# The sums over the weights woven into the raw chunks' products, and mean and variance at other places of TensorE's order

## The chip, the cores and the metric

The kernel runs on one core of one Trainium2 chip. A core has a matrix engine (TensorE, called PE in the profile; its loads of weights are called PEld), a vector engine (VectorE, DVE), an engine for functions (ScalarE, ACT), a general one (GpSimd, POOL) and one that issues the transfers (SyncE, SP). The metric is the time of one execution on the device in microseconds. Three runs of the kernel before gave 3748.06, 3753.95 and 3755.0 us, so the median is 3753.95 us.

## The reference

Two models of two layers each run one after the other on a sequence of 512 tokens of width 1024. In the first, each layer has a gated feed-forward block, a token mixer and a second feed-forward block; behind each stands a layer norm, whose result is scaled and shifted by a modulation for the next block:

```
y = _swiglu(_modulate(x, sh1, sc1), ffn1_w_gate[l], ffn1_w_up[l], ffn1_w_down[l])
x = _post_norm(x, y, g1, FFN_RES, ln_gain[l, 0], ln_bias[l, 0])      # layer norm of ALPHA*x + res_w*(1+gate)*y
y = _token_mixer(_modulate(x, sh2, sc2), w_in[l], w_out[l])
...
mu = jnp.mean(xf, -1, keepdims=True)
var = jnp.mean(jnp.square(xf - mu), -1, keepdims=True)
y = (xf - mu) * lax.rsqrt(var + LN_EPS)
```

The first model has six such norms. The change touches five: all but the last, which is followed by the second model and goes another way. What follows each of the five is a product of the modulated norm with a weight matrix, and this is what the kernel starts early: with A the product of gain and scale, and B that of bias, scale and shift, the product of h = A (x - mu) r + B with W is r (W'(A x) - mu W'A) + W'B. W'(A x) needs neither mean nor variance, and W'A and W'B are two sums over the weights per output column.

## The kernel before, in words

All activations lie transposed in the core's memory: 8 row tiles of 128 features by 512 tokens. Weights come in chunks of 8 x 128 rows by 256 columns (1 MB) into a ring of three staging tiles (`s_stage`). ScalarE rounds a chunk to its high part (`s_wh`, L1714), VectorE subtracts this from the chunk and so makes the low part (`s_wl`, L2039); activations are split the same way (`s_hh`, `s_hl`, and `s_ah`, `s_al`). A product is three products of parts, each of 512 columns (L1361, for all of TensorE's products go through one helper). The step `mm2` takes a chunk's two output tiles together: for each row tile k it issues 2 x 3 products into two banks.

A planner (class `Plan`) writes a list of steps. Each engine walks through that one list and issues its own part of each step, so the order in the list is the order on every engine. `tick()` lets background work (attention, tables) put in steps of its own. `late` (L339) is the planner's part for one of the five norms. It takes two weight chunks, `one` and `two` (gate and up of the feed-forward block, or two chunks of `w_in`), whose products are made of the raw A x (tiles `s_ah`, `s_al`), while mean and variance are still on their way. In TensorE's order there stand:

- four row tiles of `one` (24 products), `ln_mean` (one fp32 product of the running sum with a constant, 2 passes of 512 columns), the other four row tiles;
- `sums` (the step `uv`, L1487) for the first output tile of `one`: for each k an fp32 product of the raw chunk in the staging tile with two columns, A and B (2 passes each, 128x2); then `ln_var` (16 passes with one column); then `sums` for the second output tile;
- two row tiles of `two`, `ln_spread` (the reciprocal root over all 128 rows, 8 passes), the other six row tiles, and `sums` for both output tiles of `two`.

VectorE subtracts the mean from the eight tiles (`ln_sub`, L2123), ScalarE squares them, POOL and VectorE add the squares up (L2118), VectorE splits the next chunk (L2039), takes the root (`ln_root`, from L2014), splits another chunk, multiplies by the root and makes the first four tiles of h (`ln_h`, L2153, L2159, L2032), reads the sums (`uv_out`, L2134 and L2136), corrects the two raw tiles of `one` (`late`, L2143 and L2146), makes the other four tiles of h and corrects those of `two`. ScalarE copies the raw tiles out of the banks (`late_copy`, L1714 with `s_tmp<-ps`), then rounds a chunk. The running sum that the mean needs is kept by POOL (L2580). A staging tile is free for its next transfer once the low part is made and, for the two raw chunks, once the sums are read.

Here is the code that the change touches.

## Time and profile before

| | us |
|---|---|
| median of the three runs | 3753.95 |
| the profiled execution's own time | 3751.07 |
| its span (first to last instruction) | 3749.8 |
| TensorE products busy | 3607.5 (96%), 16972 |
| TensorE weight loads busy | 2925.8 (78%) |
| VectorE busy | 1844.1 (49%) |
| ScalarE busy | 1267.9 (34%) |
| POOL busy | 517.8 (14%) |
| small products of the raw chunks with the coefficients (`ps<-s_sm,s_stage`) | 43.1, 320 passes, 267 ns mean |
| ScalarE's rounding of a chunk (`s_wh`, L1714), mean of one | 1.876 |
| VectorE's split of a chunk (`s_wl`, L2039), mean of one | 2.190 |
| granted TensorE clock, mean of the span | 0.965 |

Busy times are sums over an engine's instructions and overlap between engines. Products are pipelined: one of 512 columns shows 0.39 us, but the next starts 0.23 us after it, so the distance from start to start is what a product costs. The granted clock is a share of full speed: 1.00 is 2.4 GHz, 0.50 is 1.2 GHz. "Idle before" names what ended an engine's wait.

### The profile page before, as it was taken

The numbers are of one execution on the slowest core, as the hardware profiler recorded it, in microseconds if no ns is written. First come the engines' busy times: TensorE is split into PE (matmuls) and PEld (weight loads), VectorE is DVE, ScalarE is ACT, GpSimd is POOL, SyncE is SP. The second block draws the span as 40 slices with busy tenths as digits, with TensorE's granted clock in tenths as the row PEclk, the third lists the DMA queues.
The fourth block names the chain that finished last, engine by engine and source line by source line (L and its number), as shares of the span: only waits on it lengthen the run. The fifth ranks groups of instructions, "written<-read, shape, count | busy, mean of one in ns | idle before, by whom it ended". The sixth has DMA issues, their size and how long they took to land. (4 is left out here: it accounts for less than half of the span.)

```text
span 3749.8 us, 41532 instructions
## 1 busy us (share of the span) xinstructions
PE 3607.5 (96%) x16972; PEld 2925.8 (78%) x16972; DVE 1844.1 (49%) x3196; ACT 1267.9 (34%) x1722; POOL 517.8 (14%) x448
## 2 busy tenths in 40 slices
PE   8999989999999999999999989988999999999999
PEld 7888867688888888867788877646878887787887
DVE  4545653665546544644643244775543334564332
ACT  2222461342224222552342233334442223343222
POOL 1010220110012000211210011111121111202111
PEclk9999999999999999999999989969999999999999
DMA  6444222134443443210132221101212222222222
GB/s 247 164 150 154 105 83 86 46 110 171 147 146 109 170 148 134 80 57 34 55 112 91 97 76 67 58 1 35 90 68 94 97 101 82 90 79 79 101 95 74
DMA packets 52609, 373.45 MB, mean 100 GB/s; under 512 B 5826, under 2 KB 5954, under 8 KB 9539
## 3 DMA queue, kind: packets, MB, share of 16 engines
q1 hardware_dynamic: 52418, 370.79, 27.6%
q8 instruction: 134, 2.20, 0.2%
q14 instruction: 57, 0.46, 0.0%
HBM read 368.67 MB, written 2.10 MB: 99 GB/s over the span
## 5 line engine op out<-in xcount | busy, mean ns | idle before, releaser
L1361 PE MATMUL ps<-s_hh,s_wh 128*128 128x512 f32 x2680 | 1069.5, 399 | 43.6 <-DVE s_wl L2039 16.4
L1361 PE MATMUL ps<-s_hl,s_wh 128*128 128x512 f32 x2680 | 1052.5, 393 | 0.0
L1361 PE MATMUL ps<-s_hh,s_wl 128*128 128x512 f32 x2680 | 1051.5, 392 | 0.0
L2039 DVE TENSOR_TENSOR s_wl<-s_stage,s_wh 128x2048 fp32r<-128x2048 f32 (+2 forms) x288 | 630.4, 2190 | 635.5 <-ACT s_wh L1714 635.3
L1714 ACT ACTIVATE s_wh<-s_stage 128x2048 fp32r<-128x2048 f32 (+1 forms) x277 | 519.7, 1876 | 629.2 <-PE ps L1361 500.9
L1361 PEld LDWEIGHTS ps<-s_hh,s_wh 128*128 128x128 f32 x2680 | 507.6, 189 | 180.5 <-issue 48.2
L1361 PEld LDWEIGHTS ps<-s_hh,s_wl 128*128 128x128 f32 x2680 | 507.5, 189 | 109.8
L1361 PEld LDWEIGHTS ps<-s_hl,s_wh 128*128 128x128 f32 x2680 | 508.2, 190 | 105.1 <-issue 2.1
L1361 PE MATMUL ps<-s_ah,s_wh 128*128 128x512 f32 x1376 | 544.8, 396 | 0.0
L1361 PE MATMUL ps<-s_al,s_wh 128*128 128x512 f32 x1376 | 539.9, 392 | 0.0
L1361 PE MATMUL ps<-s_ah,s_wl 128*128 128x512 f32 x1376 | 539.7, 392 | 0.0
L2615 POOL TENSOR_TENSOR s_al<-s_tmp,s_ah 128x512 fp32r<-128x512 f32 x152 | 196.7, 1295 | 1684.2 <-ACT s_ah L1714 1684.2
L1361 PEld LDWEIGHTS ps<-s_ah,s_wl 128*128 128x128 f32 x1376 | 261.0, 190 | 55.6
L1361 PEld LDWEIGHTS ps<-s_al,s_wh 128*128 128x128 f32 x1376 | 261.2, 190 | 54.9 <-issue 1.2
L1361 PEld LDWEIGHTS ps<-s_ah,s_wh 128*128 128x128 f32 x1376 | 261.2, 190 | 54.7 <-issue 1.2
L1738 ACT ACTIVATE s_tmp<-ps 128x512 f32<-128x512 f32 x146 | 87.1, 596 | 438.6 <-PE ps L1361 438.5
L1714 ACT ACTIVATE s_ah<-s_tmp 128x512 fp32r<-128x512 f32 x152 | 96.1, 632 | 407.9 <-DVE s_tmp L2234 342.8
L2092 DVE TENSOR_TENSOR s_xr<-ps,s_xr 128x512 f32<-128x512 f32 x96 | 66.2, 690 | 231.0 <-PE ps L1361 231.0
L2090 DVE SCALAR_TENSOR_TENSOR s_xr<-ps,s_sm,s_xr 128x512 f32<-128x512 f32 x112 | 83.9, 749 | 169.0 <-PE ps L1361 168.7
L2055 DVE SCALAR_TENSOR_TENSOR s_tmp<-s_stage,s_cond,s_tmp 128x256 f32<-128x256 f32 x378 | 155.3, 478 | 0.0
L2234 DVE TENSOR_TENSOR s_tmp<-s_tmp,ps 128x512 f32<-128x512 f32 x82 | 56.1, 685 | 147.9 <-PE ps L1361 147.8
L2220 DVE TENSOR_TENSOR s_tmp<-s_tmp 128x512 f32<-128x512 f32 x64 | 47.1, 736 | 165.5 <-ACT s_tmp L1738 165.4
(428 smaller groups left out, 3649.8 us busy)
## 6 DMA issues: line engine op xcount, KB each, us to landing
s_stage<-in_w_ada SPq DMA_DIRECT2D x64, 1024.0 KB, 4.8
s_stage<-in_ffn_w_gate SPq DMA_DIRECT2D x44, 1024.0 KB, 4.8
s_stage<-in_ffn_w_up SPq DMA_DIRECT2D x44, 1024.0 KB, 4.8
s_stage<-in_ffn_down SPq DMA_DIRECT2D x32, 1024.0 KB, 4.8
s_stage<-in_w_up SPq DMA_DIRECT2D x32, 1024.0 KB, 4.8
s_stage<-in_down_m SPq DMA_DIRECT2D x32, 1024.0 KB, 4.8
s_stage<-in_w_in SPq DMA_DIRECT2D x24, 1024.0 KB, 4.8
s_stage<-in_ffn_down SPq DMA_DIRECT2D x16, 768.0 KB, 4.2
```

The costliest lines, as they stand in the source:

```text
L1361: return pe.matmul(out, lhs, rhs, start=start, stop=stop, skip_group_check=True)
L1714: return act.activation(out, src, ACT.Copy)
L1738: act.activation(m.tmp(q), m.bank(b), ACT.Silu if kind == "swiglu" else ACT.Relu).then_inc(*e.up("act_ffn", "act", pid))
L2039: ins = dve.tensor_tensor(m.WL[:, ws, a:z], m.STAGE[:, j % NS, a:z], m.WH[:, ws, a:z].bitcast(F32), ALU.subtract)
L2055: ins = dve.scalar_tensor_tensor(dst, w[:, k, :], cond, dst, ALU.mult, ALU.add)
L2090: ins = dve.scalar_tensor_tensor(x, m.bank(b), m.small(gate[0])[:, n:n + 1], x, ALU.mult, ALU.add)
L2092: ins = dve.tensor_tensor(x, m.bank(b), x, ALU.add)
L2220: dve.tensor_tensor(m.tmp(q), m.tmp(q), m.tmp(q), ALU.mult).then_inc(*e.up("dve_ffn", "act.sq", pid))
L2234: dve.tensor_tensor(m.tmp(q), m.tmp(q), m.bank(b), ALU.mult).then_inc(*e.up("dve_ffn", "glu", pid))
L2615: pool.tensor_tensor(m.AL[a][:, k, :], m.tmp(q), m.AH[a][:, k, :].bitcast(F32), ALU.subtract).then_inc(*e.up("pool_a", "a.lo", av, k))
```

## The change

The sums over the weights are no longer steps of their own. `mm2` gets a further argument, and behind the six products of a row tile k it issues that row tile's share of both sums (`weight_sums`): four passes of two columns, whose weights are the raw chunk. So the 32 passes of a chunk come in eight groups of four. `ln_mean` moves from behind row tile 3 of `one` to behind row tile 1, and `ln_var` now follows the last row tile of `one` with no sums around it. `uv_out` of `one` is read ahead of `ln_root` and no longer behind the first half of `ln_h`. As the part of `one` is now handed out in three pieces and not in two, `tick()` is called once more in each of the five norms.

```diff
-        def part(ch, pid, kt, n, bs, x, ver, ks, i0, i1):
-            self.add("mm2", pid, ch, kt, n, bs, x, ver, ks, i0, i1)
+        def part(which, ch, pid, kt, n, bs, x, ver, ks, i0, i1):
+            self.add("mm2", pid, ch, kt, n, bs, x, ver, ks, i0, i1, 0, (sid, s, uv, which))
             self.tick()
-
-        def sums(ch, i, t):
-            self.add("uv", sid, ch, s, uv, i, t)
...
-        def finish(ch, i, mean, rs):
-            self.add("uv_out", sid, ch, i, uv, su)
+        def finish(i, mean, rs):
...
-        part(*one, 0, 4)
+        part(0, *one, 0, 2)
         mean = self.banks.take()
         self.add("ln_mean", sid, norm.acc, mean)
         self.tmp.free(norm.acc, ("ln.mean", sid))
-        part(*one, 4, 8)
+        part(0, *one, 2, 4)
+        part(0, *one, 4, 8)
...
         if low:
             self.add("low", *low)
-        sums(one[0], 0, 0)
         self.add("ln_var", sid, sq, var)
         for n in (3, 7):
             self.tmp.free(sq[n], ("ln.var", sid))
-        sums(one[0], 0, 1)
         self.release(one[0], ("proj", one[1] + 1))
         copies(one, 0)
+        self.add("uv_out", sid, one[0], 0, uv, su)
...
-        finish(one[0], 0, mean, rs)
-        part(*two, 4, 8)
+        finish(0, mean, rs)
+        part(1, *two, 4, 8)
         self.add("ln_h", sid, rs, s, self.hfree, self.hv, qs, 4, NT)
-        for t in range(2):
-            sums(two[0], 1, t)
         self.release(two[0], ("proj", two[1] + 1))
         copies(two, 1)
-        finish(two[0], 1, mean, rs)
+        self.add("uv_out", sid, two[0], 1, uv, su)
+        finish(1, mean, rs)
...
+            if uv:
+                weight_sums(ch, k, i == 0, i == kt - 1, *uv)
+
+    def weight_sums(ch, k, start, stop, sid, s, b, which):
+
+        w = m.STAGE[:, ch.j % NS, :].rearrange("p (k n) -> p k n", k=NT)
+        if start:
+            e.wait_ge(("ln.c", sid, 3), ("uv.out", sid, 0) if which else b.after)
+        for t in range(2):
+            at = 4 * which + 2 * t
+            ins = mul(m.bank(b)[:, at:at + 2], w[:, k, t * P:(t + 1) * P], m.small(s)[:, k:k + 9:8], start and t == 0, stop)
+        if stop:
+            ins.then_inc(*e.up("pe_uv", "uv", ch.j))
```

On TensorE, at the end of chunk `one` in the first of the five norms, there stand before (`s_sm,s_stage` are the sums, `s_cc,s_tmp 128x1` the variance, `s_ah`/`s_al` with `s_wh`/`s_wl` the raw products; here each product of fp32 counts once, in the trace it is two passes):

```order
L1361 MATMUL ps<-s_ah_70,s_wl 128x512
L1361 MATMUL ps<-s_sm,s_stage 128x2 [waits q_dve_mod]
L1361 MATMUL ps<-s_sm,s_stage 128x2 x7
L1361 MATMUL ps<-s_cc,s_tmp 128x1 [waits q_pool_sum]
L1361 MATMUL ps<-s_cc,s_tmp 128x1 x3
L1361 MATMUL ps<-s_cc,s_tmp 128x1 [waits q_dve_fold]
L1361 MATMUL ps<-s_cc,s_tmp 128x1 x3
L1361 MATMUL ps<-s_sm,s_stage 128x2 x8
L1361 MATMUL ps<-s_ah_70,s_wh 128x512 [waits q_dve_x6,q_dve_x5,q_dve_w]
```

At the same place, on TensorE, there stand now:

```order
L1356 MATMUL ps<-s_ah_70,s_wl 128x512
L1356 MATMUL ps<-s_sm,s_stage 128x2 x2
L1356 MATMUL ps<-s_cc,s_tmp 128x1 [waits q_pool_sum]
L1356 MATMUL ps<-s_cc,s_tmp 128x1 x3
L1356 MATMUL ps<-s_cc,s_tmp 128x1 [waits q_dve_fold]
L1356 MATMUL ps<-s_cc,s_tmp 128x1 x3
L1356 MATMUL ps<-s_ah_70,s_wh 128x512 [waits q_dve_x6,q_dve_x5,q_dve_w]
```

Of the 16 products for the sums two are left at this place; the others stand behind the earlier row tiles, and the ones for `two` likewise.

On TensorE, around the mean of the same norm (`s_tmp,s_cc 128x512`), there stand now two row tiles of `one` ahead of it, each with its two products for the sums; before, it stood behind four row tiles and with no sums between:

```order
L1356 MATMUL ps<-s_sm,s_stage 128x2 [waits q_dve_mod]
L1356 MATMUL ps<-s_sm,s_stage 128x2
L1356 MATMUL ps<-s_ah_70,s_wh 128x512 [waits q_dve_h]
L1356 MATMUL ps<-s_al_71,s_wh 128x512
L1356 MATMUL ps<-s_ah_70,s_wl 128x512
L1356 MATMUL ps<-s_ah_70,s_wh 128x512
L1356 MATMUL ps<-s_al_71,s_wh 128x512
L1356 MATMUL ps<-s_ah_70,s_wl 128x512
L1356 MATMUL ps<-s_sm,s_stage 128x2 x2
L1356 MATMUL ps<-s_tmp,s_cc 128x512 [waits q_dve_x4,q_pool_sum]
```

The mean thus moved ahead of two row tiles (12 products), and its own waits stay the same.

On VectorE, from the last fold of the squares to the root of the same norm, the two copies of the sums move in (a piece of the difference):

```order
 L2039 TENSOR_TENSOR s_wl<-s_stage,s_wh 128x2048
+L2134 TENSOR_SCALAR s_sm<-ps 128x2
+L2136 COPY s_sm<-ps 128x2
 L2014 TENSOR_SCALAR s_nv<-ps 128x4
 L2016 TENSOR_SCALAR s_nu<-s_nv 128x4
```

They stood between the first half of `ln_h` and the corrections of `one`. The orders of ScalarE, POOL and SyncE are the same as before.

## Rows read from the trace of the kernel before

**Rows 1.** Timeline of TensorE, norm one: start us, us, what, [idle before].

```profile
417.56 1.02 PE L1361 MATMUL ps<-s_tmp,s_cc 128*128 128x512 f32 x2
...
418.65 0.39 PE L1361 MATMUL ps<-s_al,s_wh 128*128 128x512 f32 x1
...
423.90 1.84 PE L1361 MATMUL ps<-s_sm,s_stage 128*128 128x2 f32 x16
...
427.35 1.05 PE L1361 MATMUL ps<-s_cc,s_tmp 128*128 128x1 f32 x8 [0.71 <-DVE s_tmp L2118]
...
430.89 0.77 PE L1361 MATMUL ps<-s_ah,s_wh 128*128 128x512 f32 x1
...
436.07 1.05 PE L1361 MATMUL ps<-s_cc,s_ny 128*128 128x128 f32 x8
...
445.17 3.63 PE L1361 MATMUL ps<-s_sm,s_stage 128*128 128x2 f32 x32
448.66 0.37 PE L1361 MATMUL ps<-s_wh,s_hh 128*128 128x256 f32 x1
```

**Rows 2.** TensorE in windows: stretch us, busy (count), granted clock, DMA share, GB/s.

```profile
429.00:436.00 7.00, 7.00 (x23) 0.51 0.42 150
449.00:453.00 4.00, 3.96 (x22) 0.58 0.75 291
...
545.00:549.00 4.00, 4.00 (x11) 0.57 0.02 6
2692.00:2697.00 5.00, 5.00 (x31) 1.00 0.63 211
```

**Rows 3.** Windows of 35 us, all engines, norms three and four.

```profile
1143.00:1178.00 35.00, 35.00 (x178) 30.27 (x177) 29.82 (x53) 18.40 (x26) 8.99 (x7) 0.85 0.20 74
1529.00:1564.00 35.00, 35.00 (x183) 30.92 (x182) 27.80 (x49) 17.29 (x25) 8.05 (x7) 0.83 0.15 46
```

**Rows 4.** Timeline of VectorE: first subtraction and first multiply of the norms.

```profile
418.62 0.69 DVE L2123 TENSOR_TENSOR s_xr<-s_xr,ps 128x512 f32<-128x512 f32 x1 [3.62 <-PE ps L1361]
437.16 0.69 DVE L2153 TENSOR_TENSOR s_xr<-s_xr,ps 128x512 f32<-128x512 f32 x1 [3.21 <-PE ps L1361]
775.07 0.69 DVE L2153 TENSOR_TENSOR s_xr<-s_xr,ps 128x512 f32<-128x512 f32 x1 [4.82 <-PE ps L1361]
1143.36 1.28 DVE L2123 TENSOR_TENSOR s_xr<-s_xr,ps 128x512 f32<-128x512 f32 x2 [3.62 <-PE ps L1361]
1161.07 0.69 DVE L2153 TENSOR_TENSOR s_xr<-s_xr,ps 128x512 f32<-128x512 f32 x1 [3.23 <-PE ps L1361]
1549.39 0.69 DVE L2153 TENSOR_TENSOR s_xr<-s_xr,ps 128x512 f32<-128x512 f32 x1 [4.71 <-PE ps L1361]
```

**Rows 5.** Timelines of POOL and TensorE behind the raw chunks, norms one and three.

```profile
451.44 1.28 POOL L2566 TENSOR_TENSOR s_hl<-s_tmp,s_hh 128x512 fp32r<-128x512 f32 x1 [1.08 <-ACT s_hh L1777]
...
1186.76 0.50 PE L1361 MATMUL ps<-s_hh,s_wh 128*128 128x512 f32 x1 [1.43 <-DVE s_wl L2039]
```

**Rows 6.** Timeline of TensorE: four small passes between products, and sixteen.

```profile
2610.76 0.50 PE L1361 MATMUL ps<-s_cc,s_tmp 128*128 128x1 f32 x4
...
2611.45 0.40 PE L1361 MATMUL ps<-s_hl,s_wh 128*128 128x512 f32 x1
...
2692.27 1.95 PE L1361 MATMUL ps<-s_cc,s_ny 128*128 128x128 f32 x16
```

**Rows 7.** Timelines of POOL and VectorE, norm one.

```profile
413.15 1.29 POOL L2580 TENSOR_TENSOR s_tmp<-s_tmp,s_xr 128x512 f32<-128x512 f32 x1 [1.32 <-DVE s_xr L2090]
...
442.49 0.15 DVE L2134 TENSOR_SCALAR s_sm<-ps 128x2 f32<-128x2 f32 x1
```

**Rows 8.** Timeline of ScalarE: copies of the raw tiles, norms one and three.

```profile
427.39 1.09 ACT L1714 ACTIVATE s_tmp<-ps 128x512 f32<-128x512 f32 x2 [1.54 <-DVE s_tmp L2118]
...
1152.39 1.09 ACT L1714 ACTIVATE s_tmp<-ps 128x512 f32<-128x512 f32 x2 [3.49 <-PE ps L1361]
```

**Rows 9.** Timeline of TensorE: a long stall in the attention of layer one.

```profile
544.75 1.68 PE L1361 MATMUL ps<-s_nk,s_cc 128*128 128x384 f32 x3 [2.95 <-POOL s_nk L2627]
```

More of the change, by code:

```diff
@@ L386, in late @@
             self.tmp.free(sq[n], ("ln.var", sid))
-        sums(one[0], 0, 1)
         self.release(one[0], ("proj", one[1] + 1))
         copies(one, 0)
+        self.add("uv_out", sid, one[0], 0, uv, su)
         low = self.ahead()
         two = self.begin(self.take(*names[1], ada=False, late=True), 8, S, "g", sid)
-        part(*two, 0, 2)
+        part(1, *two, 0, 2)
         y, rs = self.yr.take(), self.banks.take()
@@ L399, in late @@
         self.yr.free(y, ("ln.rs", sid))
-        part(*two, 2, 4)
+        part(1, *two, 2, 4)
         self.hv += 1
@@ L1407, in mm, with mm2 @@
             ins.then_inc(*e.up("pe_proj", "proj", pid))
-    def mm2(pid, ch, kt, N, bs, x, ver, ks, i0, i1, wait=0):
+    def mm2(pid, ch, kt, N, bs, x, ver, ks, i0, i1, wait=0, uv=None):
         wh, wl = weights(ch, kt, 256)
@@ L1485, in ln_var @@
         ins.then_inc(*e.up("pe_norm", "ln.var", sid))
-    def uv(sid, ch, s, b, i, t):
-        w, at = m.STAGE[:, ch.j % NS, :].rearrange("p (k n) -> p k n", k=NT), 4 * i + 2 * t
-        e.wait_ge(("ln.c", sid, 3), ("uv.out", sid, 0) if i else b.after)
-        for k in range(NT):
-            ins = mul(m.bank(b)[:, at:at + 2], w[:, k, t * P:(t + 1) * P], m.small(s)[:, k:k + 9:8], k == 0, k == NT - 1)
-        if t == 1:
-            ins.then_inc(*e.up("pe_uv", "uv", ch.j))
     def ln_spread(sid, y, rs):
@@ L1692, in tensor @@
     run(plan, dict(
-        mm=mm, mm2=mm2, mmt=mmt, ada_pe=ada_pe, ada_sum=ada_sum, ln_mean=ln_mean, ln_var=ln_var, uv=uv,
+        mm=mm, mm2=mm2, mmt=mmt, ada_pe=ada_pe, ada_sum=ada_sum, ln_mean=ln_mean, ln_var=ln_var,
         ln_spread=ln_spread, ln_a=ln_a, ln_last=ln_last, rms_a=rms_a, rms_b=rms_b, m_rope=m_rope, sb_z=sb_z, sb_sum=sb_sum,
```

## The prediction

> **What bounds the kernel now.** I read the page first, then TensorE's own timeline at the five layer norms that the change touches (they begin near 418, 754, 1143, 1530 and 1846 us; I call them norms one to five), then the granted clock of those stretches, then VectorE and ScalarE beside them. The page says that TensorE is busy for 96% of the span, so a change pays if it takes work off TensorE, makes that work run faster, or closes a stall. In norm one [rows 1] the reader is to see five things in order: the mean (two passes, 417.56), then 24 products of 512 columns, then a heap of small passes from 423.90 to 430.89 (16 for the sums over the weights, 16 for the variance with a wait of 0.71 us in them, 16 more for the sums), then twelve products that take 436.07 - 430.89 = 5.2 us where 24 of them took 423.90 - 418.65 + 0.23 = 5.5 us ahead of the heap (0.2275 each), then the spread of the reciprocal root at 436.07. After 36 more products a second heap of 32 passes takes 448.66 - 445.17 = 3.49 us.
>
> The windows [rows 2] say why: behind the first heap the granted clock is 0.51 for 7 us, which is the lower of the two levels (1.2 and not 2.4 GHz), and behind the second heap 0.58 over 4 us. TensorE was not idle ahead of either fall but for the 0.71 us; it ran small passes. All five norms have it: over 35 us each the mean clock is 0.85 in norm three and 0.83 in norm four [rows 3] (one and five are like three, two like four), which is (1 - 0.85) x 35 = 5.2 and 6 us of full clock lost.
>
> That is not yet what can be won, since VectorE's chain (subtract the mean, squares, variance, root, normalise, write h) hangs on TensorE at two places, mean and spread: it waits 3.62 us for the mean and 3.2 to 4.8 us for the spread in each norm [rows 4]. And what TensorE does after the two raw chunks needs that chain: in norm one the next product waits for the last h tile (POOL until 452.72), in norm three it waits 1.43 us at 1186.76 for weights that VectorE split late [rows 5]. So I count how much earlier VectorE gets its mean and its spread.
>
> **Removed, added, moved.** The number of passes is the same: 320 small ones of two columns (43.1 us busy in the table), 32 to a chunk, ten chunks. They now come in 16 groups of four per norm in place of heaps of 16, 16 and 32. Price of a group of four [rows 6]: without it the two products behind it would start 0.23 us apart, with it 2611.45 - 2610.76 = 0.69, so 0.46 us, or 0.116 a pass. The heap of 32 costs 3.49 [rows 1], or 0.109 a pass. So a group costs some 0.02 us beyond its passes, and there are 13 more groups in a norm than heaps: 65 x 0.02 = 1.3 us, all inside the sums below. These rows have other operands (a constant and a statistics tile); no row shows fp32 weights from the staging tile in fours. Bounds: from below, the first load hidden behind the product before, 0.1 us less a group (80 x 0.1 = 8 us less work); from above, twice the row, 0.9. I take the row, as the passes of both kinds show the same length in a heap of 16 (1.84 for the sums, 1.95 for a spread) [rows 1, 6].
>
> The Trainium skill (TensorE: Matmul & The Clock Gate, What happens when you issue a matmul) says that the weights of the next tile load while the running matmul streams. By that a group standing behind a long product would hide its first load, which a heap hides once for 16; the page alone would put the groups at the lower bound just named. The rows show no such discount (0.116 a pass in fours, 0.109 in thirty-two), so I don't take it.
>
> The mean moves from behind 24 products to behind 12 products and two groups: 12 x 0.2275 - 2 x 0.46 = 1.8 us earlier. It can: it needs the last running sum, which POOL finishes at 414.44 in norm one, and the mean would be at 417.56 - 1.8 = 415.8 [rows 7]. No queue of SP, ACT or POOL changes its order; on VectorE only the two small copies of the sums move ahead of the root, where VectorE has just finished a split of weights and waits for the variance; at 0.15 us each, overlapping a little, they free 0.25 us later in the chain [rows 7].
>
> From the new mean, with the clock full: mean 418.65 - 417.56 - 0.23 = 0.86; 36 products 8.19; six groups 2.78; variance 16 passes 1.75, without the 0.71 us wait, as the folds now end 1.8 us earlier and TensorE comes later: 13.6 us to the end of the variance (in norm one its second half began 427.35 - 417.56 = 9.8 after the mean and took 0.9, so 10.7, so the root starts later relative to the mean, which is the price of putting sums ahead of it). Then 12 products and two groups, 3.66: the spread starts 17.3 us after the mean, against 436.07 - 417.56 = 18.5. VectorE's first multiply follows the spread by 437.16 - 436.07 = 1.09, so it lies 17.3 us behind VectorE's first subtraction (itself 1.06 behind the mean). Before, that distance was 437.16 - 418.62 = 18.54 in norm one and 17.71 in norm three (and five, which is like it); norm two waits 4.82 for the spread and not 3.21 as norm one, so 20.15, and norm four 4.71 and not 3.23 as norm three, so 19.2 [rows 4].
>
> What is late next: in norms three to five the copies of the raw products on ScalarE wait for the variance, and not in norms one and two (1152.39 "PE", 427.39 "DVE") [rows 8]. Behind the variance stand there some 0.2 us until the copies start, 1.09 for them, 1.9 for ScalarE's rounding of a chunk and 2.2 for VectorE's split of it (both by their means in the table), 5.4 in all against the 4.75 of the spread: the distance is 17.95 in these three.
>
> Gain per norm, at VectorE's first multiply: 1.8 + 18.54 - 17.3 = 3.0; 1.8 + 20.15 - 17.3 = 4.65; 1.8 + 17.71 - 17.95 = 1.55; 1.8 + 19.2 - 17.95 = 3.05; 1.55. Sum 13.8, and with 0.25 each 15.1 us. TensorE itself would be 3.7 us and more ahead (the heap of 3.49 us becomes six groups, 2.78, and 3.4 us at half clock behind it go), but it meets the h tiles and the late weights, so the smaller number counts and the rest turns into stalls.
>
> Two terms go the other way. First, the last group and the variance still stand together: 20 small passes, 2.2 us. Sixteen together left the clock at 1.00 (2692.27, window from 2692) [rows 2, 6]; thirty-two brought it down (window from 449: (1 - 0.58) x 4 = 1.7 us of full clock lost, 3.4 us at the lower level) [rows 2]; twenty are not shown. Such a half stretch costs 1.7 us, of which norms three to five hide 0.65: 6.6 us if it comes everywhere, 0 if nowhere; I take half, 3.3. Second, the new stalls: in norms two, three and five the wait for weights grows from 1.4 to some 4 us, in one and four some 2 us of waits for h tiles arise. A stall of 2.95 us was followed by a clock of 0.57 over 4 us, again 1.7 us lost [rows 2, 9]. Up to 1.7 us each in four norms (norm three has another such wait 12 us later that hides it): 0 to 6.8, I take 2.5. In all 15.1 - 3.3 - 2.5 = 9.3 us.
>
> One small thing more: each norm now hands the background work one turn more, which moves a few small instructions of the fifth by twelve products; between -0.5 and +0.5 us, taken as 0.
>
> The profiled execution took 3751.07 us, 2.9 under the median of the three runs and 1.2 under their mean (3752.3). I set the gain against that mean: 3743.
>
> **The rivals.**
> (B) The half clock stays in another place: it comes behind all five bursts of twenty and all four new stalls. For it: heaps of 32 did it in all five norms, and so did the stall of 2.95 us [rows 9]. Against it: sixteen passes did not. 15.1 - 6.6 - 6.8 = 1.7 us gained: 3750.6, no change that can be told (about 0.2%, 7.5 us, is what a measurement of this kernel can tell).
> (C) The clock holds everywhere, 15.1 us gained: 3737. For it: between two groups stand six full products. Against it: the burst of twenty.
> (D) Slower: a group in fours costs far more than the row, since fp32 passes from the staging tile stand between fp32r products and each change of kind costs a drained array. For it: no row has these operands in fours. Against it: other small passes cost 0.46 in fours, the way back to products included [rows 6]. Ten groups stand between the first raw product and the spread on the chain, fifty in all; 15.1 us are gone when a group costs 0.30 us more than the row, and at 0.9 us (the upper bound) 50 x 0.44 = 22 us are lost against 15.1 gained: 3759.
> That the change does not do what it says (the sums would wait for a coefficient or a bank at the new place) I exclude: the coefficients are needed by the raw products anyway.
>
> (E) The clock falls between mean and spread exactly as it does now, because what brings it down is not the heaping of small passes but something that the change leaves in place. For it: nothing in one trace tells the two apart. Against it: each of the ten heaps has its own fall behind it (two in norm one) [rows 2]. Then 3.4 us are lost in norms one, three and five and 5.1 in two and four, as now, and the distances are 17.3 + 3.4 = 20.7 and 17.3 + 5.1 = 22.4: the sum of 1.8 + (distance before) - (distance after) is -4.8, with the 1.25 of the moved copies -3.5, so 3755.8.
>
> The Trainium skill (TensorE: Matmul & The Clock Gate, Why this matters for your kernels) puts a clock that drops in mid-kernel down to idle gaps between matmul bursts; by that rule the busy heaps would not be the cause and (E) would be the case. The clock falls behind the second heap too, ahead of which TensorE was busy without a wait [rows 1, 2], so the trace disagrees.
>
> **How the numbers follow.** Main case 0.47, 3743, its own range 3738 to 3748; (B) 0.20; (C) 0.18; (D) 0.10; (E) 0.05. Faster by over 0.2%, that is below 3745: all of C and two thirds of the main case, 0.50. Slower: D, 0.10. The rest, 0.40, within 0.2%. Range 3734 to 3756: it takes in C, the main case, B, E and the near side of D.
>
> **What would show each step.** Small passes in fours that lengthen the distance of two products to 0.69 us; the first subtraction 1.8 us nearer to the raw products; a clock of 1.00 between mean and spread or one half stretch of 3.4 us, and none where the heap of 32 stood; VectorE's distance of 17.3 us in norms one and two and 18 in three to five; a wait of some 4 us for weights in norms two, three and five. I am wrong if the distance stays at 18 to 20, if a group costs over 0.6 us, or if the time won at the norms comes back as waits further on.

## The result, and the profile after

The changed kernel took 3743.94 us (median of 13 runs, 3740.87 to 3751.33) where the kernel before took 3753.19 beside it: ratio 0.9979, 95% interval [0.9970, 0.9987]. Timed again later it was 0.9974 [0.9963, 0.9984] (3744.04 us, 7 runs). So it is faster by 0.2 to 0.3%. The forecast was 3743. All ratios here compare fast runs alone, so they differ a little from the quotient of two medians (0.9975 here), and one run of the kernel before that took 8327 us is in none of them.

Norm one on TensorE in the changed kernel, its small passes, with the products around the first group of four (columns as in [rows 1]):

```profile
413.54 0.39 PE L1356 MATMUL ps<-s_ah,s_wl 128*128 128x512 f32 x1
413.77 0.50 PE L1356 MATMUL ps<-s_sm,s_stage 128*128 128x2 f32 x4
...
414.45 0.40 PE L1356 MATMUL ps<-s_al,s_wh 128*128 128x512 f32 x1
...
415.97 1.10 PE L1356 MATMUL ps<-s_tmp,s_cc 128*128 128x512 f32 x2
...
427.43 0.50 PE L1356 MATMUL ps<-s_sm,s_stage 128*128 128x2 f32 x4
427.79 1.93 PE L1356 MATMUL ps<-s_cc,s_tmp 128*128 128x1 f32 x16
431.83 0.84 PE L1356 MATMUL ps<-s_sm,s_stage 128*128 128x2 f32 x4
...
434.84 1.14 PE L1356 MATMUL ps<-s_cc,s_ny 128*128 128x128 f32 x8
```

From the start of a group of four to the start of the second product behind it there are 414.45 - 413.77 = 0.68 us, as [rows 6] had it (0.69). The burst of twenty is there at 427.43. Behind it one group takes 0.84 in place of 0.50: the clock is down. The windows of TensorE in the same kernel (stretch, busy and count, granted clock, DMA share, GB/s; the answer to [rows 2, 3]) show where it falls now:

```profile
430.00:434.00 4.00, 4.00 (x14) 0.57 0.54 227
449.00:453.00 4.00, 2.80 (x19) 1.00 1.00 424
...
792.00:795.50 3.50, 3.50 (x10) 0.52 0.76 250
...
1178.00:1184.00 6.00, 5.58 (x13) 0.50 0.73 247
1514.00:1549.00 35.00, 35.00 (x198) 1.00 0.09 32
...
1878.00:1884.00 6.00, 5.53 (x13) 0.50 0.57 186
```

One half stretch of 3.4 us behind the burst of twenty in norm one (two and three have it too), none in norms four and five, none where the heap of 32 stood. In norm four the clock is 1.00 over 35 us where it was 0.83. But at 792, 1178 and 1878 us it is at the lower level. The kernel before has full clock behind the same products (norms two, three and five):

```profile
801.00:805.00 4.00, 4.00 (x18) 1.00 0.76 264
1187.00:1191.00 4.00, 4.00 (x19) 1.00 0.87 274
1890.00:1894.00 4.00, 4.00 (x19) 1.00 0.73 262
```

What stands there is the wait for late weights, grown from 1.43 us [rows 5], in TensorE's timeline of the changed kernel:

```profile
791.71 0.61 PE L1356 MATMUL ps<-s_hh,s_wh 128*128 128x512 f32 x1 [3.55 <-DVE s_wl L2039]
...
1178.42 0.80 PE L1356 MATMUL ps<-s_hh,s_wh 128*128 128x512 f32 x1 [3.53 <-DVE s_wl L2039]
...
1878.47 0.79 PE L1356 MATMUL ps<-s_hh,s_wh 128*128 128x512 f32 x1 [3.64 <-DVE s_wl L2039]
```

VectorE, the answer to [rows 4]: first subtraction and first multiply of norm one, then those of norm four, whose multiply shows no wait for TensorE:

```profile
417.12 1.28 DVE L2123 TENSOR_TENSOR s_xr<-s_xr,ps 128x512 f32<-128x512 f32 x2 [1.85 <-PE ps L1356]
436.02 0.69 DVE L2153 TENSOR_TENSOR s_xr<-s_xr,ps 128x512 f32<-128x512 f32 x1 [1.65 <-PE ps L1356]
...
1521.05 1.28 DVE L2123 TENSOR_TENSOR s_xr<-s_xr,ps 128x512 f32<-128x512 f32 x2 [1.85 <-PE ps L1356]
1538.88 0.68 DVE L2153 TENSOR_TENSOR s_xr<-s_xr,ps 128x512 f32<-128x512 f32 x1
```

Why the weights are late shows in norm two (VectorE, then ScalarE, same kernel): VectorE's split waits 2.50 us for ScalarE's rounding of the same weights, and ScalarE starts that at 787.44, behind its last tile of the raw products' silu.

```profile
789.37 2.29 DVE L2039 TENSOR_TENSOR s_wl<-s_stage,s_wh 128x2048 fp32r<-128x2048 f32 x1 [2.50 <-ACT s_wh L1714]
```

```profile
786.90 0.63 ACT L1714 ACTIVATE s_ah<-s_tmp 128x512 fp32r<-128x512 f32 x1 [1.33 <-DVE s_tmp L2224]
787.44 1.89 ACT L1714 ACTIVATE s_wh<-s_stage 128x2048 fp32r<-128x2048 f32 x1
```

Behind norm four, in the attention of layer two, one more half stretch stands that the kernel before has not: TensorE waits 1.79 us for a tile of POOL (1589.97), and then the clock is at the lower level, in the second timed execution too (1596.80:1600.00, 0.50). The kernel before waits there as long (1601.09, 1.72 us) and stays at full clock (1601.00:1605.00, 1.00). Changed kernel:

```profile
1590.80:1594.00 3.20, 3.20 (x9) 0.50 0.02 5
```

Last, the span cut at the first product of each norm's raw chunk, TensorE's windows. Kernel before:

```profile
412.12:748.43 336.31, 312.39 (x1588) 0.93 0.21 76
748.43:1136.86 388.43, 386.33 (x1755) 0.98 0.39 141
1136.86:1523.58 386.72, 383.87 (x1747) 0.99 0.39 139
1523.58:1839.88 316.30, 302.99 (x1555) 0.95 0.15 54
```

The changed kernel:

```profile
412.40:742.69 330.29, 305.40 (x1587) 0.96 0.21 77
742.69:1129.40 386.71, 383.16 (x1756) 0.99 0.39 142
1129.40:1516.34 386.94, 383.41 (x1748) 0.99 0.38 139
1516.34:1830.52 314.18, 299.30 (x1555) 0.96 0.15 54
```

The changed kernel in the second timing, another execution of the same program:

```profile
412.00:748.58 336.58, 312.12 (x1588) 0.94 0.21 76
748.58:1135.27 386.69, 383.13 (x1755) 0.99 0.39 142
1135.27:1522.30 387.03, 383.50 (x1747) 0.99 0.38 139
1522.30:1836.51 314.21, 299.35 (x1556) 0.96 0.15 54
```

The reader is to see two things. Stretches two to four repeat to 0.1 us between the two executions of the changed kernel, and there it gains 1.7, -0.2 or -0.3, and 2.1 us. The first stretch does not repeat: 330.29 and 336.58. It holds norm one and the attention of layer one, with its many short waits. By the starts of the same product, before less changed, norm one ends (477 us) 1.5 and 1.7 us ahead in the two executions, and at 559 us, in the attention, they are 3.2 ahead and 0.2 behind. What is apart there is the granted clock (0.96 and 0.94), and no instruction of the change stands there. So some 4 of the 9.2 us between the first two traces are no effect that can be put down to a place. The whole span of the second execution is 3746.5 us, only 3.3 under the kernel before. Other stretches can scatter too: in two executions of the kernel with only the mean moved (below) the stretch of norm four, with the attention of layer two, took 317.0 and 313.2 us.

### The profile page after: what moved, and what is told of

The parts are those of the page before. It is cut to its first block, busy times and chain, and to the rows that moved or that the text cites. A ratio compares the mean times of both kernels' runs of the same rounds, so it can differ in the third digit from the quotient of the medians.

```text
span 3740.6 us, 41529 instructions
## 1 busy us (share of the span) xinstructions
PE 3592.7 (96%) x16972; PEld 2912.7 (78%) x16972; DVE 1843.8 (49%) x3196; ACT 1268.0 (34%) x1722; POOL 517.8 (14%) x448
## 4 chain that ended last, share of the span: by engine, by line
PE 43%; DVE 5%; ACT 2%; issue 1%; POOL 0%; DVEq 0%; ACTq 0%; POOLq 0%
PE ps L1356 42%; DVE s_wl L2039 1%; ACT s_wh L1714 0%; ACT s_tmp L1867 0%; DVE s_tmp L2313 0%; PE ps L1381 0%; DVE s_hl L2032 0%; DVE s_tmp L2303 0%; DVE s_tmp L2209 0%; DVE s_sm L2311 0%; ACT s_hh L1714 0%; DVE s_gc L2489 0%; DVE s_tmp L2436 0%; DVE s_sm L2416 0%; DVE s_bm L2418 0%
```

## The experiments

Each is timed against the kernel before on the same chip. The experiments ran on three chips, so kernels of different experiments are best compared by their ratios. All results at a glance:

| kernel | median us (runs) | ratio, 95% interval |
|---|---|---|
| changed, again | 3744.04 (7) | 0.9974 [0.9963, 0.9984] |
| only the mean moved | 3747.24 (11) | 0.9981 [0.9972, 0.9990] |
| the same, again | 3748.09 (11) | 0.9984 [0.9975, 0.9993] |
| only the sums woven | 3754.33 (12) | 1.0005 [0.9997, 1.0014] |
| changed, a quarter of the sums' passes | 3737.31 (5) | 0.9954 [0.9942, 0.9966] |
| changed, weights split early | 3736.65 (6) | 0.9947 [0.9933, 0.9961] |
| mean moved in norms one, two only | 3750.14 (12) | 0.9999 [0.9987, 1.0011] |
| before, chunk in three parts | 3751.57 (12) | 0.9996 [0.9986, 1.0006] |
| mean moved, weights split early | 3745.10 (12) | 0.9986 [0.9976, 0.9996] |
| changed, variance in halves | 3740.44 (5) | 0.9958 [0.9945, 0.9972] |
| changed, variance in halves and weights split early | 3725.36 (6) | 0.9932 [0.9918, 0.9947] |

**The change taken apart.** My theory was that weaving brings most of the gain, by keeping the clock up, and the mean's move little.

Only the mean moved:

```diff
-        part(*one, 0, 4)
+        part(*one, 0, 2)
...
         self.add("ln_mean", sid, norm.acc, mean)
...
+        part(*one, 2, 4)
         part(*one, 4, 8)
```

> The kernel before with one edit: the mean stands behind two row tiles of the first raw chunk and no longer behind four; the sums stay in their heaps of 16, 16 and 32 passes. Theory (the gain of the change comes from the earlier mean and the full clock together, and neither alone carries it): VectorE's first subtraction comes 12 x 0.2275 = 2.7 us earlier against the raw chunk, but the 12 products now stand behind the mean, so the variance and the spread stay where they were on TensorE; only the wait of 0.71 us inside the heap goes in norms one and two, and the half clock behind both heaps stays. Gain 1.4 us in all, ratio to before 0.9996, no difference that can be told; distance from first subtraction to first multiply 20.5 us in norm one where it was 18.5. Rival (the earlier mean is what wins the time, the weaving is idle): five times 1.8 to 2.7 us, 9 to 13 us, ratio 0.997.

Measured 0.9981: the theory's number is missed, the rival's is met. The mean comes 5.44 - 2.72 = 2.7 us earlier, the folds come in time, and the variance no longer waits in the heap. Below are TensorE's heaps of norm two in this kernel, and the clock behind them:

```profile
756.62 1.84 PE L1362 MATMUL ps<-s_sm,s_stage 128*128 128x2 f32 x16
758.32 2.12 PE L1362 MATMUL ps<-s_cc,s_tmp 128*128 128x1 f32 x16
760.30 3.55 PE L1362 MATMUL ps<-s_sm,s_stage 128*128 128x2 f32 x16
```

```profile
759.00:767.00 8.00, 8.00 (x36) 0.57 0.25 80
```

Half stretches stay behind both heaps. What the trace shows as gained is the wait of 0.71 us in the heaps of norms one [rows 1] and two, and one half stretch fewer between mean and spread in norms one, two and four (one more in norm three). In a second execution of this kernel norm one has as much of it as before; two, three and four are as here.

Only the sums woven, the mean in its old place:

```diff
         part(0, *one, 0, 2)
+        part(0, *one, 2, 4)
...
         self.add("ln_mean", sid, norm.acc, mean)
...
-        part(0, *one, 2, 4)
         part(0, *one, 4, 8)
```

> The changed kernel with one edit: the mean goes back behind four row tiles of the first raw chunk; the sums stay woven in groups of four. Theory: the mean comes 7.3 us after the start of the raw chunk where the changed kernel has 3.6, the squares are summed 9.7 us after it, TensorE gets to the variance after 8.2 and waits 1.5 us, with half of the variance done in the wait; the multiply comes 22.8 us after the start of the raw chunk at full clock and 24.5 with one half stretch behind the variance, where it was 25.1 in norm one, 26.7 in two, 24.2 in three and five and 25.7 in four before, and is 22.0 to 23.6 in the changed kernel. Gain 3 to 7 us against before, ratio 0.9985, that is about half of the change. Rival (the weaving alone does it, the place of the mean is idle): the ratio of the changed kernel, 0.9979. Rival (the earlier mean does it): 1.000.

Measured 1.0005: missed as well. In norm one of this kernel four groups stand ahead of the mean, which comes 7.23 us behind the raw chunk's start and not 5.44, and the folds, later by as much, are waited for:

```profile
419.69 1.11 PE L1356 MATMUL ps<-s_tmp,s_cc 128*128 128x512 f32 x2
...
429.56 1.67 PE L1356 MATMUL ps<-s_cc,s_tmp 128*128 128x1 f32 x8 [0.67 <-DVE s_tmp L2118]
```

The clock does not hold either: between mean and spread it is at the lower level for 6.8 us in norms one to three and 3.4 in four and five, and behind the variance TensorE waits 0.5 to 1.15 us in each norm for weights that VectorE, now later, splits later. Sum by places: VectorE's first multiply is 26.4 us behind the raw chunk's start against 25.0 before in norm one, and 24.7 against 25.8 in norm four; the stalls for the weights are 3.5 us all the same, with half clock behind them. So the mean alone gives some 6 us, the weaving alone none, both together 8 to 10. The reading that fits the traces is that the earlier mean pays for the groups ahead of it, and the weaving needs the earlier mean. But the intervals of the mean alone and of both overlap, so what weaving adds in this setting is not shown.

**What limits the change.** Two candidates: the price of the groups, and the stall behind the norms.

The sums at row tiles 0 and 7 only (240 of the 320 passes are left out, so the sums are incomplete):

```diff
-            if uv:
+            if uv and i in (0, kt - 1):
                 weight_sums(ch, k, i == 0, i == kt - 1, *uv)
```

> The changed kernel, and of the eight groups of four small passes of each raw chunk only the first and the last are issued: six of eight row tiles are left out of the two sums over the weights, so 240 of 320 passes go. It measures what a group costs on the chain. Theory (a group costs 0.46 us on TensorE, and TensorE sets the mean and the spread): of the ten groups ahead of the spread seven go (row tile 0 and 7 of the first chunk and row tile 0 of the second stay), 3.2 us; the multiply comes up to 3.2 us earlier in each norm, less where ScalarE's copies and rounding set it; the 20 passes around the variance stay and with them the chance of a half stretch. 8 to 16 us faster than the changed kernel, ratio to before 0.994 to 0.996. Rival (a group in fours with fp32 weights from the staging tile costs 0.9 us): 25 to 30 us faster, 0.990. Rival (groups are hidden, the chain sits elsewhere): within 2 us of the changed kernel, 0.998.

Measured 0.9954 [0.9942, 0.9966], in the range of the ratio that the theory gave; the gain over the changed kernel is 6.6 us by the medians and 9 by the ratios, at the lower end of the 8 to 16 expected. The 240 passes are 60 groups, so 60 x 0.46 = 28 us of TensorE's time went, and only a quarter to a third of it came out as time. VectorE's multiply comes 13.0 us earlier over the five norms, but TensorE then waits behind the variance (0.67 us in norms one and two) and at the h tiles (1.74 and 1.21 us in norm one), and the stall for weights stays (3.64 us in norm two). So the groups do cost something, and most of what they cost is hidden.

The weights behind the norms split early. This adds one item to the order, so that ScalarE's rounding and VectorE's split of the next chunk stand ahead of the raw products' silu:

```diff
                     one, two, afree[1] = self.late(norm, ((names["gate"], idx), (names["up"], idx)))
+                    low = self.ahead()
+                    if low:
+                        self.add("low", *low)
```

> The changed kernel with one edit: in the three norms in front of a feed-forward block, the chunk that TensorE waits for after the third (3.5 us in norms two, three and five) is rounded and split right behind the raw chunks, ahead of the activation and the parts of the first output tiles, and not behind them. Theory (what the change won at the norms is partly given back by this wait and by the half clock behind it): ScalarE's rounding comes some 7 us earlier, the wait of 3.5 us goes in norms two and five, in norm three at least in part (its next chunk is behind a transfer), and so does the half stretch that follows it (lost clock 1.7, 3.4 and 3.4 us there). Gain over the changed kernel 3 x 3.5 + 3 to 5 = 8 to 15 us, ratio to before 0.994 to 0.996. Rival (the wait is only moved: the activation and its parts come later and TensorE waits for them or for the transfer): ratio 0.998 as the changed kernel.

Measured 0.9947 [0.9933, 0.9961], in the expected range: 7 us under the changed kernel by the medians (just short of the 8 expected) and 12 by the ratios, for an edit without any work less. Its six runs lie from 3725.9 to 3741.6 us, and the profiled one is the fastest, so the trace as a whole flatters it; single stretches tell more. The stretch of norm two has no stall and only the half stretch behind the burst of twenty (first row); in norm three, where the chunk behind the next is one of modulation weights, which is not split this way, the edit gives way and the stall of 3.64 us stays (second row):

```profile
739.54:1120.79 381.25, 381.25 (x1755) 1.00 0.39 144
1120.79:1506.58 385.79, 381.98 (x1747) 0.99 0.38 139
```

Against 386.71 of the changed kernel that is 5.5 us in norm two alone: the wait of 3.55 and the half stretch behind it, 1.7, are 5.25 of them.

**Was it the mean after all?** Mean alone had met the whole change. Three kernels look at it. First, the mean moved in norms one and two only:

```diff
+        if self.nlate <= 2:
+            part(*one, 0, 2)
+        else:
+            part(*one, 0, 4)
```

> The kernel before, and the mean stands behind two row tiles of the first raw chunk in norms one and two alone; norms three to five and all sums as before. With the mean moved in all five the ratio to before was 0.9981 (6 to 7 us), where I had worked out 1.6 us from the trace (the wait of 0.71 us inside the heap, norms one and two) and some 1 us of clock. Theory A (the wait in the heap is all that the earlier mean can remove, and with it one half stretch more is spared now and then): the whole gain is in norms one and two, so this run has the ratio of the mean moved in all five, 0.998 to 0.9995. Theory B (the earlier mean wins in every norm, since VectorE and ScalarE are done earlier and something behind them starts earlier): two fifths of it, 0.9992, and the distance from raw chunk to multiply in norm three to five is shorter only where the mean moved. In both the raw chunk to multiply is 24.2 us in norms one and two with a fall of 6.8 us, 22.6 with one of 3.4 us.

Measured 0.9999 [0.9987, 1.0011]. That is outside the range of Theory A, but the interval reaches into it and holds B's number, so it does not tell the two apart.

Second, the kernel before with `one` in three parts and the mean where it was (`part(*one, 0, 2)`, `part(*one, 2, 4)`, mean, `part(*one, 4, 8)`), which hands the background work its one turn more and does nothing else:

> The kernel before, and the first raw chunk's products are handed out in three pieces and not in two, with the mean still behind the fourth row tile: TensorE's, VectorE's and the other orders at the norms stay as before, only the background work gets one turn more per norm, which shifts some of its instructions behind the fifth norm. Theory: no effect, ratio 1.000 within its interval. Rival (a part of what the moved mean brought, 0.9981, is the further turn): 0.999 or less.

Measured 0.9996 [0.9986, 1.0006]: the extra turn is worth nothing that can be told, as the prediction took it.

Third, mean moved and weights split early, with the sums in heaps (the two diffs above on the kernel before):

> The kernel before with the mean moved in all five norms (0.9981) and the chunk behind the third rounded and split ahead of the activation in front of the feed-forward blocks, with the sums in heaps, not woven. The woven kernel with the same early split has 0.9947. Theory (weaving saves time on the chain, and its gain is given back in the wait for that chunk; where the wait is gone the gain shows): this one keeps the heaps' half stretches, 6.8 us and 3.4 us a norm, saves the waits of 1.4 us in norms two and five, and stays some 5 to 8 us behind the woven one, ratio to before 0.9965 to 0.9975. Rival (weaving is worth nothing whatever stands behind it): 0.9947 as with the woven sums.

Measured 0.9986 [0.9976, 0.9996], less gain than expected; the rival's 0.9947 is out. With the stall out of the way the weaving is worth 0.9986 against 0.9947, about 15 us (the ends of the intervals allow 6 to 24); with the stall in place the intervals of mean alone and of the whole change overlap (0.9981 and 0.9984 against 0.9979 and 0.9974). Read the other way, the early split brings nothing that can be told to the kernel with heaps (0.9981 and 0.9984 to 0.9986), whose wait is 1.4 us, and 0.003 to the woven one, whose wait is 3.5. The two early-split kernels show in norm two's stretch what weaving holds: 384.20 us with heaps, 381.25 woven, and neither waits.

```profile
740.75:1124.95 384.20, 384.20 (x1755) 0.99 0.40 143
```

Then the mean alone and the changed kernel once more, side by side:

> The kernel with only the mean moved, timed once more beside the changed kernel itself, to settle whether the mean's move alone brings what the whole change brings. Theory (moving the mean gains 1.8 us of VectorE's start per norm, but the heap of small passes waits in norms one and two for the folds, and half clock shifts by chance of where the stretches fall; the true gain is 3 to 5 us): 0.9986 to 0.9993. Rival (it brings as much as the whole change, as its first timing said): 0.9975 to 0.9984, equal to the changed kernel.

> The changed kernel, timed once more beside the kernel with only the mean moved on the same chip. Both theories: 0.9975 to 0.9985 of the kernel before, as at the first timing (0.9979); the scatter between chips or launches would show as a time outside these.

Measured 0.9984 [0.9975, 0.9993] and 0.9974 [0.9963, 0.9984]. The changed kernel repeats. The mean alone lies in the rival's range at its upper edge, and its interval reaches into the theory's range too; two timings put it at 6 to 7 us. Its two traced executions are only 3.9 and 3.0 us shorter than that of the kernel before. They show 1.4 us of waits less in the heaps of norms one and two. Norm two's stretch is 385.96 us in both executions, 2.5 less than before, norm three's 388.30 and 388.69, 1.6 and 2.0 more. What the rest of the 6 to 7 us is stays open.

**A version that beats both.** Changed kernel, early split, in norm three also past the chunk of modulation weights, and the variance in two halves, behind the sixth and the seventh row tile, so that nowhere 20 small passes stand together:

```diff
-        part(0, *one, 4, 8)
+        self.add("mm2", *one[1:2], one[0], *one[2:], 4, 6, 0, (sid, s, uv, 0))
...
-        self.add("ln_var", sid, sq, var)
+        self.add("ln_var", sid, sq, var, 3)
+        self.add("mm2", *one[1:2], one[0], *one[2:], 6, 7, 0, (sid, s, uv, 0))
+        self.add("ln_var", sid, sq, var, 7)
...
+        part(0, *one, 7, 8)
```

> A version meant to beat both: the changed kernel with the early split (0.9947), the same early split also over a chunk of the modulation weights (norm three), and the variance in two halves of eight passes, one behind the sixth and one behind the seventh row tile of the first raw chunk, so that no more than 12 small passes stand together. Theory (the 20 passes around the variance bring a half stretch in three of five norms, 1.05 to 1.7 us each; the wait of 3.6 us in norm three and the 6.8 us of half clock behind it go): the distance from first subtraction to first multiply is 17.3 to 17.8 us in all five norms, no fall between mean and spread, norm three's wait shorter by 3 us; 4 to 8 us faster than the woven kernel with the early split, ratio to before 0.9925 to 0.9935. Rival (the clock falls behind 12 passes too, or the norms' distance is set by ScalarE's copies): 0.9947.

Measured 3725.36 us, 0.9932 [0.9918, 0.9947]: 25.9 us under the kernel before on that chip. It is clearly faster than the kernel before and than the changed kernel; its interval overlaps that of the changed kernel with the early split (0.9947). TensorE in norm one: bursts of 12 passes, and the clock of norms one to three in one window each (the windows of 48 us of four and five read 1.00 as well):

```profile
422.56 0.50 PE L1364 MATMUL ps<-s_sm,s_stage 128*128 128x2 f32 x4
422.92 1.03 PE L1364 MATMUL ps<-s_cc,s_tmp 128*128 128x1 f32 x8
...
425.66 1.03 PE L1364 MATMUL ps<-s_cc,s_tmp 128*128 128x1 f32 x8
```

```profile
413.00:448.00 35.00, 34.10 (x198) 1.00 0.16 59
744.00:792.00 48.00, 48.00 (x254) 1.00 0.24 88
1125.00:1173.00 48.00, 48.00 (x252) 1.00 0.24 88
```

One part of the expectation failed: norm three's wait is not shorter by 3 us. It only stands further on, and what ended it is another cause. The split weights come late because ScalarE waits 5.76 us for the transfer of the next `gate` chunk (TensorE, then ScalarE):

```profile
1181.46 0.50 PE L1364 MATMUL ps<-s_hh,s_wh 128*128 128x512 f32 x1 [3.46 <-DVE s_wl L2046]
```

```profile
1177.16 1.92 ACT L1721 ACTIVATE s_wh<-s_stage 128x2048 fp32r<-128x2048 f32 x1 [5.76 <-DMA s_stage<-in_ffn_w_gate]
```

The half clock behind it is 3.4 us and no longer 6.8. In all, norm three's stretch is 384.07 us where the changed kernel has 386.94 and the one with the early split alone 385.79.

The same without the early split, to part the two edits:

> The changed kernel with one edit: the variance in two halves of 8 small passes, the first behind the sixth row tile of the chunk and the second behind the seventh, so that no burst of 20 small passes stands between mean and spread; the early split of weights is left out. Theory (the half stretch of 3.4 us between mean and spread in norms one, two and three comes from the burst of 20; without it VectorE's spread comes 1.1 to 1.5 us earlier there, but where weights are split late it only lengthens the stall, and a longer stall brings half clock): distance first subtraction to first multiply about 17.4 us in all five, no low clock between mean and spread, stalls for the split weights of 3.5 us and more still in norms two, three and five with half clock behind them; time 0.996 to 0.998 of the kernel before, hardly better than the changed kernel. Rival (the burst is the larger loss and the stall behind the norms does not matter): 0.9935 to 0.995, near the kernel with both edits (0.9932).

Measured 0.9958 [0.9945, 0.9972], between the theory (0.996 at best) and the rival (0.995 at worst), and nearer the theory. The distance from first subtraction to first multiply is 17.37 us in all five norms and no half stretch stands between mean and spread; the stalls for weights remain (3.62 us at norms two and three, 3.64 at five) with half clock behind them. Its stretch of norm two is 385.98 us, 0.7 under the changed kernel; with the early split it is 379.65. Windows of TensorE without it and with it:

```profile
742.17:1128.15 385.98, 382.36 (x1756) 0.99 0.39 142
```

```profile
743.57:1123.22 379.65, 379.65 (x1755) 1.00 0.40 144
```

## Why the prediction was right

The number was met (a median of 3743.94 where 3743 was said), and the chain up to VectorE's multiply came out nearly as worked out. What follows behind it did not, and so the hit is in part luck.

**The groups of four.** Held: 0.68 us where 0.69 was said. The hidden first load, the lower bound, did not show, and (D) is out.

**The mean.** 415.97 - 412.40 = 3.57 us behind the raw chunk's start, before 417.56 - 412.12 = 5.44: 1.87 earlier, 1.8 said.

**The distance.** Said 17.3 in norms one and two and 17.95 in the others, half stretches apart. Measured 1538.88 - 1521.05 = 17.83 in norm four, the same in five; 436.02 - 417.12 = 18.90 in norm one, with its half stretch, and 17.30 in norm one of the kernel with the early split, where none fell.

**The burst of twenty.** The term was half of 6.6 us, 3.3. It brought a half stretch in three norms of five, and these have VectorE's first multiply 23.6 us behind the raw chunk. Without one it is 22.54 us in norms three to five, and 22.01 in norm one of the kernel with the early split: 2 x 1.6 + 1.05 = 4.3 us, norm two taken like norm one. Which norms it hits is not settled by the burst: with the early split the same bursts brought it in norm two alone. Over all five, the multiply came 1.4, 3.0, 0.6, 3.3 and 1.65 us earlier (25.04 to 23.62 in norm one, and so on), 10.0, and 11.2 with the copies' 0.25 each; the prediction's own sum up to here is 15.1 - 3.3 = 11.8.

**The new stalls: the term that was mis-sized.** Said some 4 us in norms two, three and five and 2 in one and four; measured 3.55, 3.53, 3.64, and 1.5 and 2.0. The loss by half clock behind them was put at 2.5 us in all, of 0 to 6.8. Norm one had none (449:453 at 1.00) and gave nothing back: counted from its chunk's start it is still 1.8 and 1.6 us ahead at 477 us. But two had 3.4 us of it, three and five 6.8 us each, which is 1.7 + 3.4 + 3.4 = 8.5 us of full clock. Norm two won 3.0 + 0.25 at the multiply and its stretch shortened by 1.7: 1.6 given back. Norm three won 0.9 and its stretch grew by 0.2: 1.1, its later wait of 1.4 us having hidden the rest. In norm five the same product, 56 us behind the raw chunk's start, stands at 1895.10 before and at 1886.52 now, 8.6 ahead, where the chunk itself was 1839.88 - 1830.52 = 9.4 ahead: nothing of the 1.9 won is left and 0.8 more is gone, 2.7. Norm four won 3.3 + 0.25 and its stretch shortened by 2.1: 1.4 given back, and the half stretch in the attention (1590.80, costing 1.7) is what stands there. The prediction has no term for it. In sum 1.6 + 1.1 + 1.4 + 2.7 = 6.8 and not 2.5.

**The total.** With 6.8 the sum at the norms is 11.2 - 6.8 = 4.4 us, where 9.3 was said. The medians show 9.2 and 10.8, the ratios 8 and 10. The first trace has its 9.2 us of span only with the 4 us of the attention stage that the second execution, 3.3 us under the kernel before, does not have. So the forecast hit with this one term more than twice too small, and with some 5 us the other way that no place in the traces accounts for. That medians over 13 and 7 runs show 5 to 6 us more than the norms' sum is open: the attention's clock may on average be better behind the new norms, but no run here shows it.

**The rivals.** (B) said half clock behind all bursts and all stalls: three of five bursts, and three of five stalls. (C) needed a clock that holds: the kernel with halves and early split comes near that case, with no half clock from mean to spread, and takes most of the stalls as well; it has 0.9932, 25.9 us and not (C)'s 15. (E) said that the clock falls between mean and spread as before. It does not in norms four and five, where the distance is 17.83 us and not 22.4 and 20.7; in norms one to three one half stretch is left where there were two or three. Where the heap of 32 stood in norm one the clock stays at 1.00 (449:453) where it was 0.58 [rows 2]. With the variance in halves nothing of (E) is left in any norm. (The prediction's own sum for (E) is -4.6 by its distances and not -4.8, so 3755.6; nothing hangs on it.) The Trainium skill (TensorE: Matmul & The Clock Gate, Why this matters for your kernels) puts a clock that drops in mid-kernel down to idle gaps between bursts of products. Both show here: behind heaps of small passes without a wait of TensorE (759:767 at 0.57, only the mean moved), and behind stalls of 3.5 us (1178:1184 at 0.50, changed kernel). That section names the second only; the measurement decides.

## What to carry to other kernels

Small passes in a heap cost more than their own time: the half clock behind them. Spread them in fours between full products, but not ahead of what a chain waits for (woven alone, with the mean late, the gain was nil), and look at the granted clock behind every burst. But first ask who will be late when TensorE is early: here the gain of weaving went into a wait for weights that two engines split too late, and came out (from 0.9979 to 0.9947) by moving that split ahead, without any work less. And cut the trace at fixed places of the program, in two executions: a stretch that repeats to 0.1 us can tell a change of 2 us, while the span of one execution carries a scatter of 6. Which stretches repeat has to be looked at each time; those with the attention in them did not always.

## What the hardware showed that was not expected

Bursts of 20 small passes (2.2 us) brought the lower clock in three of five norms of the changed kernel, the same three in both executions, but with the early split in one of five (norm two); bursts of 12 in none of ten (two kernels with the variance in halves); heaps of 32 (3.5 us) in all five of the kernel before. Waits of about 3.5 us were followed by 3.4 us at the lower level in some places and 6.8 in others, in the same kernel and with the same products behind them. Shorter waits are not safe either: waits of 1.4 us in norms two, three and five of the kernel before were followed by none, but the wait of 1.8 us behind norm four was in both executions of the changed kernel, while 1.7 us at the same product was not in the kernel before. In the kernel with the variance in halves alone, 3.4 us of it follow waits of 0.32 and 1.18 us in norm one (450.2:453.4 at 0.50), which are followed by none in the changed kernel. Two executions of one program were 6.3 us apart in one stage of 330 us and within 0.1 us in the three behind it; of another program they were 3.8 us apart in the stage of norm four.
